# Rows of the shared experts loaded in quarters and turned on VectorE for all tiles but the last of each layer

## What is computed

```
h2 = modulate(rms_norm(x, norm_ffn), sh2, sc2)
scores = sigmoid(h2 @ router_w)                  # 16 experts, top 2 of one group
out = (silu(h2 @ ws_gate) * (h2 @ ws_up)) @ ws_down          # the shared expert, width 256
for e in range(16):
    out = out + gates[:, e:e+1] * swiglu(h2, w_gate[e], w_up[e], w_down[e])
x = x + g2 * out
```

## Time and profile before

| | |
|---|---|
| median of 3 runs | 1561.45 us (1559.13 to 1563.37) |
| the profiled execution | 1559.23 us, its span 1557.4 us |
| busy: PE, DVE, ACT, POOL | 97%, 56%, 25%, 19% of the span |
| granted TensorE clock, mean | 0.994 of full |
| DMA | 283.52 MB, mean 182 GB/s |

### The profile page before, as it was taken

The page is one execution under the profiler, slowest core; times in us unless marked ns, Lnnn a source line. Parts: engine busy times, 40 slices in busy tenths (PEclk is TensorE's granted clock), DMA queues, the critical chain, the costliest instruction groups (busy, mean ns, idle before and its releaser), DMA issues.

```text
span 1557.4 us, 25671 instructions
## 1 busy us (share of the span) xinstructions
PE 1504.9 (97%) x9630; PEld 1004.2 (64%) x9630; DVE 879.2 (56%) x1828; ACT 396.0 (25%) x886; POOL 302.8 (19%) x464
## 2 busy tenths in 40 slices
PE   6999999999999999999999999999999999999995
PEld 4655445766665577678887555556666667688883
DVE  2323523567676667667766721524567766765556
ACT  1322113455554420000000412113455541000001
POOL 0111101000000000555542110201000000265532
PEclk9999999999999999999999999999999999999998
DMA  9642111640011297699998871113711026489994
GB/s 359 202 154 108 55 51 65 217 150 17 25 41 42 73 325 270 221 330 365 365 358 306 290 256 55 55 51 118 254 60 42 14 81 219 167 312 339 339 360 170
DMA packets 104938, 283.52 MB, mean 182 GB/s; under 512 B 20404, under 2 KB 34268, under 8 KB 95080
## 3 DMA queue, kind: packets, MB, share of 16 engines
q1 hardware_dynamic: 91728, 261.03, 46.9%
q0 software_dynamic: 12528, 21.03, 3.7%
q10 hardware_dynamic: 584, 0.14, 0.0%
HBM read 262.52 MB, written 38.53 MB: 193 GB/s over the span
## 4 chain that ended last, share of the span: by engine, by line
PE 86%; DVE 5%; DMA 4%; issue 3%; POOL 1%; ACT 1%; SPq 0%; DVEq 0%; POOLq 0%; ACTq 0%
PE S L1292 18%; PE S L1670 14%; PE B L1458 9%; PE S L1378 8%; PE S L1681 7%; PE PT L1399 6%; PE B L1435 6%; PE B L1313 3%; PE B L1196 3%; PE S L1313 2%; DMA arena<-in_w_mod 2%; DVE arena L2287 1%; PE S L1549 1%; PE PT L1260 1%; DMA arena<-h,arena 1%
## 5 line engine op out<-in xcount | busy, mean ns | idle before, releaser
L1292 PE MATMUL S<-arena 128*128 128x512 f32 (+3 forms) x768 | 296.3, 536 | 2.7 <-ACT arena L965 2.7
L1670 PEld LDWEIGHTS S<-arena 128*128 128x128 f32 x2304 | 263.4, 192 | 23.3 <-issue 23.3
L1670 PE MATMUL S<-arena 128*128 128x128 f32 x2304 | 264.4, 275 | 4.9 <-DVE arena L2565 3.1
L1292 PEld LDWEIGHTS S<-arena 128*128 128x128 f32 x768 | 139.8, 190 | 123.2 <-issue 102.3
L1072 ACT ACTIVATE arena<-S,nmax 128x768 f32<-128x768 f32 (+1 forms) x200 | 155.0, 778 | 144.8 <-DVE nmax L2165 120.6
L1847 POOL DMA_INDIRECT arena<-h,arena x144 | 148.1, 1028 | 172.3 <-issue 105.8
L2165 DVE TENSOR_REDUCE nmax<-S 128x1 f32<-128x768 f32 (+1 forms) x168 | 133.2, 826 | 70.6 <-PE S L1378 60.5
L1458 PE MATMUL B<-arena 128*128 128x512 f32 x320 | 153.7, 602 | 0.6 <-DVE arena L2223 0.5
L1378 PE MATMUL S<-arena 64*128 64x256 f32 (+5 forms) x624 | 135.2, 473 | 2.2 <-ACT arena L1072 2.2
L1681 PE MATMUL S<-arena 128*128 128x512 f32 x288 | 129.6, 592 | 0.0
L1399 PEld LDWEIGHTS PT<-cst,arena 128*128 128x128 f32 x768 | 86.9, 141 | 65.2 <-issue 51.7
(11 more groups left out here) (322 smaller groups left out, 1677.2 us busy)
## 6 DMA issues: line engine op xcount, KB each, us to landing
arena<-in_w_mod SPq DMA_DIRECT2D x24, 2048.0 KB, 10.5
arena<-in_moe_w_gate SPq DMA_DIRECT2D x36, 1024.0 KB
arena<-in_moe_w_up SPq DMA_DIRECT2D x36, 1024.0 KB
arena<-in_moe_w_down SPq DMA_DIRECT2D x36, 1024.0 KB
arena<-in_w_in SPq DMA_DIRECT2D x6, 2048.0 KB, 8.2
arena<-y SPq DMA_DIRECT2D x20, 512.0 KB, 6.5
arena<-mod SPq DMA_DIRECT2D x16, 512.0 KB, 6.7
arena<-in_tokens SPq DMA_DIRECT2D x12, 512.0 KB, 9.3
```

The costliest lines, as they stand in the source:

```text
L1292: mm = pe.matmul(ubank[u % 4][:, c0:PANEL_W[p]], hT[:, k, t * P:(t + 1) * P], panel[p][:, k, c0:], start=k == 0, stop=k == KT - 1)
L1670: mm = pe.matmul(to, wgu[b][:, w, k * DE + h * P:k * DE + (h + 1) * P], XT[b][:, k, :], start=k == 0, stop=k == KT - 1)
```

## The change

`hs_load` issues four DMAs per tile instead of one. DMA f takes columns 256f to 256f+255 of the 128 rows and puts them on partitions 32f to 32f+31, each partition getting four pieces of 1 KB (from rows i, 32+i, 64+i, 96+i). So each DMA moves 128 KB in 128 pieces and writes 32 partitions. DVE `s_half(t)` for t below nt-1 is now one stream transpose of 128x1024 from these rows to `hT2[t]`; it waits for the loads itself. PE's `s_turn` and ACT's `s_half` are left for the last tile alone; PE's three waits that guarded PSUM stand after the output pieces, and `s_turn(nt-1)` follows `s_gate(nt-3)`. Two waits of SP and POOL that said "all rows turned" (`s_tr`) now watch `s_t_v`, DVE's count. Tiles affected: five in layer 0, three in layer 1.

```
--- before.py
+++ after.py
@@ -783,7 +783,9 @@
                     sp.dma_start(h2_d[l][rows, :], h2b).then_inc(s["h2_stored"], 16)
 
                 def hs_load(t):
-                    sp.dma_start(hs_of[l][t], h2_d[l][span(t * P, P), :]).then_inc(s[f"hs_in{int(t >= 2)}"], 16)
+                    rows = h2_d[l][span(t * P, P), :].rearrange("(a i) (f c) -> f i a c", a=4, f=4)
+                    for f in range(4):
+                        sp.dma_start(hs_of[l][t][32 * f:32 * f + 32, :].rearrange("p (a c) -> p a c", a=4), rows[f]).then_inc(s[f"hs_in{int(t >= 2)}"], 16)
 
 
 
@@ -853,7 +855,7 @@
                     down_load(b, e)
 
 
-                sp.wait_ge(s["s_tr"], gend)
+                sp.wait_ge(s["s_t_v"], gend)
                 if l == 0:
                     mod_rows(1, 0, LATE, (0,))
                     mod_load(1, 2, 0)
@@ -1126,11 +1128,8 @@
 
                 def s_half(t):
 
-                    act.wait_ge(s["s_tr"], g(t) + 1)
-                    if t == 2:
-
-                        act.wait_ge(s["h2_ready"], gend)
-                    act.activation(hT2[t][:, 4:8, :].rearrange("p a b -> p (a b)"), (S1 if t == 1 else PT)[:, 512:1024], ACT.Copy).then_inc(s["s_t_s"], 1)
+                    act.wait_ge(s["s_tr"], l + 1)
+                    act.activation(hT2[t][:, 4:8, :].rearrange("p a b -> p (a b)"), PT[:, 512:1024], ACT.Copy).then_inc(s["s_t_s"], 1)
 
                 def s_exp(t):
 
@@ -1142,15 +1141,13 @@
                     act.wait_ge(s["s_ht"], g(t) + 1)
                     act.activation(hidT[t % 2].rearrange("p a b -> p (a b)"), B7[:, 0:DE], ACT.Copy).then_inc(s["s_hts"], 1)
 
-                s_half(0)
-                s_half(1)
                 x1_square(nt - 1)
                 if l == 0:
 
                     act.wait_ge(s["h2_ready"], gend)
                 for t in range(2, nt):
                     s_exp(t - 2)
-                    s_half(t)
+                s_half(nt - 1)
 
                 for t in range(nt - 2, nt):
                     s_exp(t)
@@ -1514,30 +1511,17 @@
 
                 def s_turn(t):
 
-                    if t == 0:
-
-                        pe.wait_ge(s["pt_v"], V_EVACS * gend)
-                        pe.wait_ge(s["pt_s"], S_EVACS * gend)
-                        pe.wait_ge(s["exp_done"], 2 * NS * gend)
-                    if t == nt - 1:
-
-                        pe.wait_ge(s["h2_ready"], gend)
-                    else:
-                        group = int(t >= 2)
-                        pe.wait_ge(s[f"hs_in{group}"], (0, (32, 16 * (T - 3))[group])[l] + (32, 16 * (nt - 3))[group])
-                    if t >= 2:
-
-                        pe.wait_ge(s["s_t_v"], g(1 if t == 2 else t))
-                        pe.wait_ge(s["s_t_s"], g(1 if t == 2 else t))
+                    pe.wait_ge(s["h2_ready"], gend)
                     x8 = hs_of[l][t].rearrange("p (n k) -> p k n", k=KT)
                     for j in range(KT):
-                        tr = pe.transpose((S1 if t == 1 else PT)[:, j * P:(j + 1) * P], x8[:, j, :], ident)
+                        tr = pe.transpose(PT[:, j * P:(j + 1) * P], x8[:, j, :], ident)
                     tr.then_inc(s["s_tr"], 1)
 
                 def s_gate(t):
 
                     pe.wait_ge(s["s_t_v"], g(t) + 1)
-                    pe.wait_ge(s["s_t_s"], g(t) + 1)
+                    if t == nt - 1:
+                        pe.wait_ge(s["s_t_s"], l + 1)
                     for k in range(KT):
                         mm = pe.matmul(gbank[t][:, 0:SW], hT2[t][:, k, :], swg[:, k, :], start=k == 0, stop=k == KT - 1)
                     mm.then_inc(s["s_g"], 1)
@@ -1598,17 +1582,18 @@
 
                 ge = lambda b: b + NBK[0] * l
 
-                s_turn(0)
-                s_turn(1)
                 for piece in range(KT, 2 * KT):
                     out_piece(nt - 1, piece)
+                pe.wait_ge(s["pt_v"], V_EVACS * gend)
+                pe.wait_ge(s["pt_s"], S_EVACS * gend)
+                pe.wait_ge(s["exp_done"], 2 * NS * gend)
                 pe.wait_ge(s["s_w_in"], 16 * 4 * (l + 1))
                 for t in range(nt):
                     if t < 2:
                         pe.wait_ge(s["res_mul"], 2 * gend - 1 + t)
                     s_gate(t)
-                    if t + 2 < nt:
-                        s_turn(t + 2)
+                    if t + 3 == nt:
+                        s_turn(nt - 1)
                 s_up(0)
                 s_up(1)
                 if l == 0:
@@ -1868,7 +1853,7 @@
                     pool.indirect_dma_start(out=y_d[l], in_=yb[b], in_offset=None, bounds_check=TOPK * nt * P - 1, oob_is_err=False,
                                             out_offset=bass.IndirectOffsetOnAxis(ap=idx2[n], axis=0)).then_inc(e_stored[l][b], 16)
 
-                pool.wait_ge(s["s_tr"], gend)
+                pool.wait_ge(s["s_t_v"], gend)
                 def first_gather(b):
 
                     if l:
@@ -2276,8 +2261,14 @@
 
                 def s_half(t):
 
-                    dve.wait_ge(s["s_tr"], g(t) + 1)
-                    dve.tensor_copy(hT2[t][:, 0:4, :].rearrange("p a b -> p (a b)"), (S1 if t == 1 else PT)[:, 0:512]).then_inc(s["s_t_v"], 1)
+                    if t == nt - 1:
+                        dve.wait_ge(s["s_tr"], l + 1)
+                        dve.tensor_copy(hT2[t][:, 0:4, :].rearrange("p a b -> p (a b)"), PT[:, 0:512]).then_inc(s["s_t_v"], 1)
+                        return
+                    group = int(t >= 2)
+                    dve.wait_ge(s[f"hs_in{group}"], 4 * ((0, (32, 16 * (T - 3))[group])[l] + (32, 16 * (nt - 3))[group]))
+                    dve.transpose(hT2[t].rearrange("p k (a i) -> p a k i", a=4),
+                                  hs_of[l][t].rearrange("p (a j k) -> p a k j", a=4, k=KT)).then_inc(s["s_t_v"], 1)
 
                 def gate_mul(m, gi, gx, gates):
```

## The result

The changed kernel takes 1567.99 us (median of 8 runs, 1564.91 to 1571.91) against 1561.39 us of the kernel before (8 runs, 1558.52 to 1565.03): ratio 1.0045 [1.003, 1.006], which is +7.0 us by the ratio. So the two profiles differ by some 4 us more than the medians.

A forecast was written before the change was run, and what follows sets the result against it. PE and DVE were taken to arrive nearly together in layer 0, the h2 chain and then PE to bound layer 1. Layer 0 +5.2, layer 1 +1.0, clock +2.5 make +8.7 us on the median: 1570.2, range 1563.5 to 1574.0.

The forecast's parts named there:

- PE and DVE's prices: Both seams: PE saves 0.89 us a tile, 1.78 for two; a DVE transpose takes 2.04 us, 1.96 in a row.
- Half rate for the quarters: Loads of h2 into 32 partitions run at 213 GB/s instead of 396; three tiles take 7.4 us instead of 4.0.
- 32 partitions at half rate as the whole cost of the loads: Both layers' h2 loads: half rate is the narrower limit; +2.2 us for two tiles, +3.4 for three, +1.2 for one.
- issue time hides under it: SP's h2 load issues, 0.43 us each, feed 305 GB/s, so half rate is narrower and hides them.
- The backlog in layer 0: Layer 0: all queued behind the first two tiles' loads, x1 store included, comes 2.0 us later; tile 2's transpose starts at 570.0.
- Layer 0 in all: Layer 0 seam: late loads +2.1, three transposes +4.05, closed gap -0.95; +5.2 us, bounds +2.6 and +7.
- Layer 1: Layer 1 seam: g2 lands late at 1306.5 and delays h2_scale and s_gate(2); +1.0 us, bounds -0.6 and +1.5.
- The clock: Layer 1: PE idles 3.3 us, its clock falls and PE is the bound; +2.5 us, bounds 0 and 3.4.
- full-rate rival: Quarters load at full rate, leaving DVE's own work: +2.6 and about +0.3, +2.9 us, 1564.4; chance 0.18.
- the clock holds, +6.2: Same as the forecast, but PE's clock does not fall in layer 1: +6.2 us, 1567.7; chance 0.22.

The follow-up runs named there:

- e2: Changed kernel, but a tile's four DMAs each take 256 columns into all 128 partitions, in 1 KB pieces: 1568.06 us, 1.0038 of the kernel before.
- f1: The change in layer 0 alone, layer 1 as in the kernel before: 1563.89 us, 1.0025 of the kernel before.
- f3: Kernel before with the change in layer 1 alone, and there rb and g2 queued ahead of the third h2 tile: 1563.30 us, 1.0015 of the kernel before.
- e4: Changed kernel, with PE running products nobody reads after s_gate(1), 10 in layer 0 and 7 in layer 1: 1568.75 us, 1.0047 of the kernel before.
- e1: Changed kernel, but each tile loaded by one DMA of 128 rows of 4 KB, DVE still turning: 1559.42 us, 0.9996 of the kernel before.
- the last version: Kernel before, tiles 0 and 1 turned on DVE from quarters laid out at h2's store, one DMA per load, layer 1's g2 ahead of third tile: 1561.63 us, 1.0010.

## Why the prediction was right, and where its steps were off

The forecast was +8.7 us, 1570.2; measured are 1567.99 and +7.0 [4.7, 9.4]. The main line held: PE's saving buys nothing, as DVE, its loads and the h2 chain bound the seams. By its steps, with times of the changed kernel's profile given less the 0.56 us (layer 0) or 8.09 us (layer 1) by which its seams start late:

- **PE and DVE's prices.** 1.78 us a layer, DVE at 2.04 a transpose, 3.91 for two in a row: as forecast.
- **Half rate for the quarters.** Right: 216 GB/s at a share of 1.17 where 213 at 1.04 was the model.
- **The step that failed: 32 partitions at half rate as the whole cost of the loads, with "issue time hides under it".** In the changed kernel issue time does hide: the last quarter lands 6.8 us after its issue. But e2 has no narrow DMA, goes at the rate of SP's issues, and loses as much in total. An issue costs 0.475 us and not the 0.43 that I took; the second line of the earlier trace rows has it, 1.38 us for three, where I had read the first.
- **The backlog in layer 0.** The x1 store landed 3.4 us late (558.74 against 555.38) where I had 2.0, and DVE then waited 0.70 for the residual, so that `h2_shift` ended at 570.4 and not 568.5. SP's wait for the h2 store at L777 grew by 2.7 (4.0 to 6.7), again where I had 2.0, so that the third tile's loads were issued at 560.35 against 557.67. The transposes of tile 2 start at 572.4 and not 570.0, 12.0 us behind the first of their issues, where I had 10.3.
- **Layer 0 in all:** DVE reached L2325 7.5 us late, the turn of the hidden rows came 7.5 late, forecast 5.2. By the medians of f1 it is 3.9 [2.2, 5.6], so that 5.2 is within and 7.5 is not. Between the routed experts of layer 0 and the seam of layer 1 the profiles vary by 10 us (642.4 to 652.1) among kernels that do the same there, so where f1's seam of +5.9 became +3.9 can't be read from one profile of each.
- **Layer 1:** g2 landed at 1306.9 (forecast 1306.5), `h2_scale` started at 1309.1 (1308.75), `s_gate(2)` at 1313.7 (1313.2): +1.5 where I had +1.0. That is this profile; the same code varies by 2.8 us among profiles. Whether the third tile ahead of g2 holds it up is not shown: f3, with g2 first, is no better. A reading of mine was inexact too: the 0.55 us at 1311.22 end with ACT's copy of tile 2 (L1133 in the earlier trace rows), which itself waits for the last h2.
- **The clock.** It fell where I said it would: a mean of 0.60 from 1319 to 1323 us of its profile in layer 1 and of 0.52 from 572 to 579 in layer 0, each with a stretch at 0.50. I charged 2.5 us for layer 1; e4 keeps the clock at 1.00, and turn and gates take 0.7 us less. By the profiles this term was about four times too large, since `s_gate(2)` waits for DVE's transpose nearly as long.

By totals the forecast's parts compare so. Without the narrow loads I expected +2.9 (the full-rate rival); e1 gave -0.6 [-2.7, 1.2]. The loads and what hangs on them, the clock included, were then 5.8 us; the changed kernel less e1 is 7.6, with some 3 us of uncertainty. So the number was near partly by luck: DVE's own work and the clock were sized too large, the loads and their backlog, it seems, too small. The rival "the clock holds, +6.2" was nearer in size, though the clock fell. The forecast called the way, the half rate and the waits rightly, and not what share each had.

## What to carry to other kernels

Before work is taken off an engine that shows no gap, look at what it would wait for if it came earlier: here a landing that came 0.2 us before it was needed made 1.8 us of saving worthless. A load cut into several DMAs has two prices: the rate of its transfers (half, at 32 partitions a DMA here) and the rate at which one engine issues them (128 KB per 0.475 us here). The slower one counts, and mending it alone uncovers the other, as e2 did. The bill comes at every store and load queued behind it, among them waits of the issuing engine for a landing, which shift the start of all later transfers. And where a layout is needed, make it at a time when no stage waits for it (with four extra stores a tile during attention the last version's total is 1.0010 [0.9999, 1.0021]), not in the load that a stage waits for.

## What the runs showed of the hardware that I had not expected

- DMAs of 128 KB with 1 KB pieces into all 128 partitions moved 260 and 275 GB/s at shares of 0.80 and 0.82, no more than SP issued (one per 0.475 us, 276 GB/s); DMAs of 512 KB with the same pieces moved 364 at 1.08, with 4 KB pieces 390 at 0.99.
- 32 partitions a DMA: 216 GB/s at a share of 1.17 with 1 KB pieces, 249 at 1.06 with 4 KB, of which 231 where the queue was full.
- PE's granted clock fell to its lower level (0.50) around 5.39 us of idleness in layer 0 and 3.71 in layer 1, and filling the gap with products kept it at 1.00 without a gain that the total shows.
- The same loads in the same place took visibly different times from profile to profile (layer 1 seam 40.6 to 43.4), more than most differences that I wanted to see there.
